# Later turns for the second modulation's weight units, and the last feed-forward unit in two halves

## The reference, cut to what matters

```python
sh1, sc1, g1, sh2, sc2, g2 = adaln(c, w_ada, b_ada)        # silu(c) @ w_ada + b_ada, split in six
h = modulate(y, norm1_w, sh1, sc1)                          # rms_norm(y) * (1 + sc1) + sh1
q, k, v, u, g = project_mixers(h, w_in, q_norm_w, k_norm_w)
att = diff_attention(q, k, v, lam, subln_w, lam_init)
sgu = spatial_gating(u, g, sgu_norm_w, w_s, b_s)
y = y + g1 * (concatenate([att, sgu]) @ w_o)
h = modulate(y, norm2_w, sh2, sc2)
y = y + g2 * (square(relu(h @ w_ff1)) @ w_ff2)
```

## Time and profile before

| what | us |
|---|---|
| median of 3 runs (2461.22 to 2461.75) | 2461.25 |
| the profiled execution | 2461.3 |
| its span (core 7, the slowest) | 2459.1 |
| spans of the eight cores | 2451.1 to 2459.1 |
| TensorE busy | 2356.5 |
| VectorE busy | 1066.5 |
| ScalarE busy | 721.3 |
| POOL busy | 207.4 |

### The profile page before, as it was taken

One profiled execution on the slowest core, in us unless ns is written; L12 is line 12 of the kernel. 1 busy time (PEld: TensorE's weight loads), 2 busy tenths in 40 slices (PEclk: granted clock), 3 DMA queues, 4 the chain that ended last, 5 costly groups with the idle time before them and its releaser, 6 DMA issues.

```text
span 2459.1 us, 38418 instructions; the slowest of 8 cores (2451.1 to 2459.1 us)
## 1 busy us (share of the span) xinstructions
PE 2356.5 (96%) x16224; PEld 1351.2 (55%) x16224; DVE 1066.5 (43%) x2129; ACT 721.3 (29%) x1185; POOL 207.4 (8%) x376
## 2 busy tenths in 40 slices
PE   2578999999999999999999999999999999999999
PEld 2367888787888854444444444444444444444444
DVE  2148763754732153553101332322524626528347
ACT  3056675765746561322231001001010010010110
POOL 2101121121100030000110000000000000000000
PEclk7679999999999999999999999999999999999999
DMA  9995786886625186966562222222433423323346
GB/s 208 171 218 156 110 118 94 110 115 111 101 50 83 32 135 140 255 202 129 87 108 52 52 52 52 52 52 52 90 65 64 90 52 75 80 50 81 64 94 188
DMA packets 168728, 251.56 MB, mean 102 GB/s; under 512 B 101104, under 2 KB 106864, under 8 KB 154480
## 3 DMA queue, kind: packets, MB, share of 16 engines
q0 software_dynamic: 54240, 164.94, 39.0%
q1 hardware_dynamic: 114320, 84.17, 13.9%
HBM read 348.28 MB, written 32.67 MB: 155 GB/s over the span
## 4 chain that ended last, share of the span: by engine, by line
PE 92%; DMA 5%; ACT 1%; another core or an unknown queue 1%; DVE 0%; POOL 0%; issue 0%; DVEq 0%; POOLq 0%
PE ps L454 92%; DMA ada<-wa 3%; DMA wr<-wa 1%; DMA xt<-xs 1%; ACT xn L487 0%; PE ps L464 0%; ACT hT L487 0%; POOL ada L575 0%; ACT P L487 0%; DVE xn L516 0%; DVE hT L516 0%; POOL wr L575 0%; ACT mod L487 0%; ACT st L497 0%
## 5 line engine op out<-in xcount | busy, mean ns | idle before, releaser
L454 PE MATMUL ps<-wf,aT 128*128 128x512 bf16 x3072 | 665.0, 379 | 0.0
L454 PE MATMUL ps<-hT,wf 128*128 128x512 bf16 x3072 | 665.0, 379 | 0.0
L454 PEld LDWEIGHTS ps<-hT,wf 128*128 128x128 bf16 x3072 | 300.4, 98 | 362.2 <-issue 0.8
L454 PEld LDWEIGHTS ps<-wf,aT 128*128 128x128 bf16 x3072 | 300.1, 98 | 362.5 <-issue 0.8
L487 ACT ACTIVATE tm<-ps 128x512 f32<-128x512 f32 x192 | 114.3, 597 | 1029.4 <-PE ps L454 1029.4
L454 PE MATMUL ps<-wr,hT 128*128 128x256 bf16 x3072 | 373.7, 277 | 6.9 <-DVE hT L516 4.6
L509 DVE TENSOR_TENSOR aT<-tm 128x512 bf16<-128x512 f32 x192 | 132.7, 692 | 548.8 <-ACT tm L487 546.0
L487 ACT ACTIVATE P<-ps 128x1024 bf16<-128x1024 f32 x304 | 295.8, 1020 | 128.9 <-PE ps L454 128.6
L454 PEld LDWEIGHTS ps<-wr,hT 128*128 128x128 bf16 x3072 | 297.3, 100 | 55.1 <-issue 18.5
L509 DVE TENSOR_TENSOR acc<-acc,ps 128x512 f32<-128x512 f32 x216 | 148.4, 687 | 157.5 <-PE ps L454 156.5
L454 PE MATMUL ps<-VV,P 128*128 128x129 bf16 x2432 | 164.1, 220 | 0.1
(11 more groups left out here) (144 smaller groups left out, 1460.7 us busy)
## 6 DMA issues: line engine op xcount, KB each, us to landing
wf<-wf POOLq DMA_DIRECT2D x64, 1024.0 KB, 8.5
wr<-wa POOLq DMA_DIRECT2D x96, 256.0 KB, 7.5
ada<-wa POOLq DMA_DIRECT2D x32, 512.0 KB, 44.0
xt<-xs POOLq DMA_DIRECT2D x14, 1024.0 KB, 8.2
wr<-wqkv POOLq DMA_DIRECT2D x48, 256.0 KB, 11.6
x1d<-xw SPq DMA_DIRECT2D x12, 1024.0 KB, 5.3
x1b<-x1d SPq DMA_DIRECT2D x48, 256.0 KB, 3.7
wo<-wo POOLq DMA_DIRECT2D x32, 256.0 KB, 15.7
```

The costliest lines, as they stand in the source:

```text
L454: ins = e.matmul(o, lhsT=l, rhs=r, start=st, stop=sp, skip_group_check=True)
```

## The change

`ADA_SLACK` goes from 2000 to 4000 ns, for the 24 units and for the later 8. The last unit of the feed-forward part is computed as two units of 256 columns, each in a bank of its own and with a multiplication, an addition and a store of its own. A parameter `lat` of `mm` is added and keeps its old value everywhere.

```diff
-ADA_SLACK = 2000.0
+ADA_SLACK = 4000.0
...
-        def out2(j, rd, nb, tt, op):
+        def out2(j, rd, nb, tt, op, c0=0, n=512):
             r = 0 if tt < 4 else 1
-            c = slice(nb * 512, (nb + 1) * 512)
+            c = slice(nb * 512 + c0, nb * 512 + c0 + n)
...
                 tf = yield tms
-                yield S.tt(tf, bank(j), g2_t[:, r, c], ALU.mult)
+                yield S.tt(tf[:, 0:n], bank(j)[:, 0:n], g2_t[:, r, c], ALU.mult)
                 banks.give(j)
-                yield S.tt(acc[:, tt, c], acc[:, tt, c], tf, ALU.add)
+                yield S.tt(acc[:, tt, c], acc[:, tt, c], tf[:, 0:n], ALU.add)
                 tms.give(tf)
                 if rd == 7:
                     S.store(yrows(tt)[:, c], acc[:, tt, c], "acc%d" % tt)
...
-                    b = yield banks
-                    op = S.mm([(bank(b), aT[:, fc, tt * 128:(tt + 1) * 128], W[:, fc, :], fc == 0, fc == 7) for fc in range(8)])
-                    S.spawn(out2(b, rd, nb, tt, op), 20)
+                    for c0, n in ((0, 512),) if (rd, nb, tt) != (7, 3, 11) else ((0, 256), (256, 256)):
+                        b = yield banks
+                        op = S.mm([(bank(b)[:, 0:n], aT[:, fc, tt * 128:(tt + 1) * 128], W[:, fc, c0:c0 + n], fc == 0, fc == 7) for fc in range(8)])
+                        S.spawn(out2(b, rd, nb, tt, op, c0, n), 20)
```

More of the change, by code:

```diff
@@ L449, in is_ps, with mm @@
         return self.tens[ap.tensor.name][0] == "p"
-    def mm(self, ops, mode="full", cost=None, prio=None):
+    def mm(self, ops, mode="full", cost=None, prio=None, lat=LAT["pe"]):
         def fn(e):
@@ L458, in mm @@
         return self.post("pe", cost, lambda: self.add("pe", fn, reads=[x for o in ops for x in (o[1], o[2])],
-                                                      writes=[o[0] for o in ops]), LAT["pe"], mode=mode, prio=prio)
+                                                      writes=[o[0] for o in ops]), lat, mode=mode, prio=prio)
     def tr(self, ops, ident):
```

## The result

The changed kernel takes 2476.4 us (median of 5 runs, 2475.4 to 2479.0), against 2461.6 (2461.2 to 2462.8) for the kernel before, run beside it: a ratio of 1.0061, 95% interval 1.0047 to 1.0075. It is slower by 15 us, three times what a measurement can tell apart. The forecast was 2460.4, within 2458.9 to 2463.2: no difference.

A forecast was written before the change was run, and what follows sets the result against it. TensorE was taken as almost always busy, leaving only 3.75 us of middle-stretch gaps and 3.7 us after the last matmul. -2.05 + 1.1 = -0.95 on core 7, a little less on core 0: 2461.3 - 0.9 = 2460.4 us, range 2458.9 to 2463.2.

The forecast's parts named there:

- The modulation waits, -2.05 us: Middle stretch, 277.7 to 740 us: TensorE's waits of 0.69, 1.20 and 0.16 us before modulation units go, on core 7.
- The tail, +1.1 us: After the last matmul: the two half stores go in turn, changing the end by 2L - 2.51, so +1.1 us.
- L = 1.8: Last unit's stores: assumed 1.8 us from issue to landing of each 128 KB half, within bounds 1.6 to 2.2.
- What is late next: Units end later, 24 by some 70 us, last 8 by some 20; cover over 400 us; moved projection weights cost nothing.
- The rival of SP: SP's queue: `gpart` store waits up to 8.8 us delay a transpose and TensorE stands; 2469.2 us, chance 0.04.
- The waits move: Middle stretch: other traffic meets other units' loads, about as much is lost, only the tail counts; 2462.4 us, chance 0.13.

The follow-up runs named there:

- scores put off: Changed kernel with last unit whole, planner counting a Q tile usable 10 us after its transpose's modelled landing (pairs 1 to 3); ratio to before 0.9989.
- split alone: Kernel before (slack 2000) with only the last unit split in two halves; ratio to before 1.0000.
- slack alone: Changed kernel with its last feed-forward unit whole again, so only the slack of 4000; 2474.9 us, ratio to before 1.0043.
- put off with own semaphore: Changed kernel, Q tiles counted usable 10 us later by the planner, second half's store on its own semaphore; ratio to before 0.9990.
- slack 6000: Kernel before with `ADA_SLACK` 6000 instead of 2000, last unit whole; ratio to before 0.9998.

## Why the prediction was wrong

- **The modulation waits, -2.05 us: right, with some luck in the size.** No core of the changed kernel or of the one with the scores put off waits for `wr<-wa`, and (A) of the latter is 2.5 us below before in the median (3.2 on core 7). Part of that is not this term: cores 1, 3, 4 and 6 did not wait for `wr<-wa` before and gained 1.7 to 2.5 us too, as their waits for `tm`, 0.6 to 1.3 us, went.
- **The tail, +1.1 us: right on seven cores, undersized on the slowest.** The stores do go in turn. On seven cores each half landed in 1.8 to 2.0 us, as L = 1.8 had it, and the tail is 4.6 to 4.8 us, the 4.8 that the prediction gave. On core 7 the halves took 2.8 and 1.8, which makes +2.1 by the prediction's formula; it came to +1.8, since the first half's sum was ready 1.1 us after the last whole unit's, not 1.35. In the split alone the first half took 2.8 to 3.0 us on four cores; why a core is slow there is open.
- **"What is late next": here it failed.** The paragraph followed the moved loads to those who wait for them (the units, the gate, the projection weights) and put the rest at nothing. Its distances were low (the 24 units end 86 us later, at 746.9, for the 70 given, the last 8 units 31 us later for 20), but nothing waits for those. It did not ask what else is on the DMA engines where a moved load arrives. Two transposes had 1.6 us to spare, and the two waits for them made the 12.5 us, with 4.2 us more at the lower clock. That a transpose lands late beside weight loads stood in the trace of the kernel before, in rows that the prediction does not have: the next two Q transposes of the same pair there, issued at 535.13 and 541.06 behind a modulation load at 532.13 and projection weights at 534.21, and waited for by nobody.

```profile
L586 SPq DMA_TRANSPOSE QT<-kr x2: 1785/1864/1943, 535.1 to 541.1; - x2
...
DMA to landing us min/median/max: 13.3/14.3/15.4
```

- **The rival of SP, 2469.2 us at 0.04: right victim, wrong mechanism.** It had TensorE stand for a transpose that SP gives out late. SP gave it out at 525.75, where 6.2 us of cover was left, and its longest wait for a `gpart` store went from 8.8 us to 4.1. And what I held against it, that TensorE "waited for no transpose in the same arrangement before", says nothing of an arrangement that the change alters. In the new order 40 + 16 projection matmuls of 0.114 us, 6.4 us, stand ahead of those scores, and that is the cover; with a landing of 13.3 us, as beside the same kinds of load in the kernel before, that is a wait of some 7 us at the first place. It measured 6.8.
- **"The waits move", 2462.4 us at 0.13**, named the shared engines, but took as victims only other units' loads, with about the same loss. The Trainium skill, page DMA: Bandwidth & Descriptors, section "Issuing engines are not separate DMA queues", says that transfers issued from different engines run on the same 16 DMA engines and interleave. The trace agrees: on core 7 SP's transpose lands in 2.5 us with no load ahead of it and in 9.7 behind one weight load of GpSimd's queue, and from 530.5 to 538.5 us of the changed kernel the two queues moved 649 and 640 packets.
- **The clock** stood in no case. Behind the two waits it cost 4.2 us more on core 7.

## What to carry to other kernels

When a change moves a transfer, list every small transfer that now overlaps it and has a waiter. Take from the trace of before how long each has from landing to first use, and how late the same kind of transfer lands where a load does overlap it. Here a spare of 1.6 us did not survive a weight load that went out ahead. A slack that only a planner sees shifts all that follows it, so its effect is not monotone: read the new order at the tight places instead of trusting the size of the constant, and give the waiter more cover rather than moving the load. Where the slowest core changes from run to run, measure from the first instruction that the change can touch.

## What the runs showed of the hardware that I had not expected

The same transpose of one Q tile, 128 KB, landed in 2.3 to 3.1 us on the eight cores of the kernel before and in 8.5 to 13.0 us in the changed one, and what changed most around it are the weight loads. With the same loads at the same distances it also differs from core to core. In the four runs that have both loads there (changed, slack alone, put off, put off with own semaphore), of the cores 0 and 1, 2 and 3, 4 and 5, 6 and 7 the one that starts its first modulation unit later in its span has the longer landing, in all 16 pairs: 9.2 us on core 3 and 12.8 on core 2, for one. Why is open.

And the same wait can cost the clock or not. With slack 6000, TensorE stood 2.27 us on core 1 and 2.34 us on core 7 at the same place; the timelines of core 1, then of core 7:

```profile
531.50 1.04 PE L454 MATMUL ps<-QT,KT 64*128 64x256 bf16 x8 [2.27 <-DMA QT<-kr]
532.47 3.85 PE L454 MATMUL ps<-wr,hT 128*128 128x256 bf16 x24
```

```profile
530.35 0.61 PE L454 MATMUL ps<-QT,KT 64*128 64x256 bf16 x8 [2.34 <-DMA QT<-kr]
530.89 2.79 PE L454 MATMUL ps<-wr,hT 128*128 128x256 bf16 x24
```

On core 1 the same matmuls took 0.43 + 1.06 = 1.5 us longer, and the granted clock of 520 to 540 us is 0.91; on core 7 it is 1.00. Of the four cores that waited 2.2 to 2.5 us there three fell (1, 3 and 5). Why core 7 did not is left open.
